# The narrow tile of the mixer shares its chunks with the third pooled tile; row totals, pooling weights and v's turn at other places of the queues

## The reference

```python
mod = (silu(c) @ ada_w + ada_b).reshape(B, 3, 3, 1024)
shift, scale, gate = mod[:, :, 0], mod[:, :, 1], mod[:, :, 2]
h = rms_norm(x, norm_g[0]) * (1 + scale[:, 0]) + shift[:, 0]
x = x + 0.5 * gate[:, 0] * swiglu(h, ffn1_w_in, ffn1_w_out)
h = rms_norm(x, norm_g[1]) * (1 + scale[:, 1]) + shift[:, 1]
x = x + gate[:, 1] * token_mixer(h, mix_w_in, conv_w, a_log, dt_bias, ..., pool_w, pool_scale, pool_proj, ...)
h = rms_norm(x, norm_g[2]) * (1 + scale[:, 2]) + shift[:, 2]
x = x + 0.5 * gate[:, 2] * swiglu(h, ffn2_w_in, ffn2_w_out)
return rms_norm(x, final_g)
```

## Time and profile before

| | us |
|---|---|
| median of 3 runs | 1915.85 (1915.74 to 1916.16) |
| the profiled execution | 1915.09 |
| its span in the profile | 1913.3 |
| PE busy | 1873.1 (98%) |
| DVE busy | 988.9 (52%) |
| ACT busy | 815.8 (43%) |
| POOL busy | 124.2 (6%) |

### The profile page before, as it was taken

The page is one execution under the profiler, slowest core; times in us unless marked ns, Lnnn a source line. Parts: engine busy times, 40 slices in busy tenths (PEclk is TensorE's granted clock), DMA queues, the critical chain, the costliest instruction groups (busy, mean ns, idle before and its releaser), DMA issues.

```text
span 1913.3 us, 22366 instructions
## 1 busy us (share of the span) xinstructions
PE 1873.1 (98%) x8923; PEld 1452.5 (76%) x8923; DVE 988.9 (52%) x1764; ACT 815.8 (43%) x1325; POOL 124.2 (6%) x148
## 2 busy tenths in 40 slices
PE   7999999999999999999999999999999999999997
PEld 4666666666788788888886777677888878888886
DVE  4566667666544643333347566854434673333322
ACT  5466556656643342222324555434432342222221
POOL 0111111110001000000010011000000100000000
PEclk9999999999999999999999999999999999999999
DMA  5334334332233132222223222221023322322221
GB/s 213 147 144 150 137 143 155 143 144 99 78 118 123 69 110 99 94 96 92 99 95 117 93 72 88 84 94 34 34 96 113 121 89 99 99 93 97 97 93 62
DMA packets 56526, 201.95 MB, mean 106 GB/s; under 512 B 6478, under 2 KB 6934, under 8 KB 55784
## 3 DMA queue, kind: packets, MB, share of 16 engines
q1 hardware_dynamic: 44616, 158.32, 23.6%
q0 software_dynamic: 11808, 42.21, 6.1%
HBM read 195.23 MB, written 5.28 MB: 105 GB/s over the span
## 4 chain that ended last, share of the span: by engine, by line
PE 76%; DVE 12%; ACT 9%; issue 2%; DMA 1%; POOL 0%; DVEq 0%; SPq 0%; ACTq 0%
PE ps L1111 22%; PE ps L1114 22%; PE ps L1112 22%; ACT wH L1820 2%; DVE wL L1404 2%; PE ps L1209 2%; PE ps L1173 1%; DVE a L1533 1%; PE ps L1197 1%; DVE a L1699 1%; ACT a L1931 1%; PE ps L1185 1%; PE ps L1245 1%; PE ps L1144 1%; DVE b L1464 1%
## 5 line engine op out<-in xcount | busy, mean ns | idle before, releaser
L1111 PE MATMUL ps<-hH,wH 128*128 128x512 f32 x1592 | 649.3, 408 | 7.6 <-ACT wH L1820 5.9
L1114 PE MATMUL ps<-hH,wL 128*128 128x512 f32 x1592 | 623.7, 392 | 0.2 <-DVE wL L1404 0.2
L1112 PE MATMUL ps<-hL,wH 128*128 128x512 f32 x1592 | 622.6, 391 | 0.0
L1404 DVE TENSOR_TENSOR wL<-wr,wH 128x1024 fp32r<-128x1024 f32 (+2 forms) x285 | 345.1, 1212 | 526.7 <-ACT wH L1820 526.5
L1820 ACT ACTIVATE wH<-wr 128x1024 fp32r<-128x1024 f32 (+2 forms) x285 | 295.0, 1036 | 239.8 <-PE ps L1114 226.1
L1111 PEld LDWEIGHTS ps<-hH,wH 128*128 128x128 f32 x1592 | 299.7, 188 | 104.6 <-issue 36.2
L1114 PEld LDWEIGHTS ps<-hH,wL 128*128 128x128 f32 x1592 | 299.0, 188 | 66.2 <-DVE wL L1404 1.1
L1112 PEld LDWEIGHTS ps<-hL,wH 128*128 128x128 f32 x1592 | 300.0, 188 | 62.6 <-issue 6.2
L1111 PE MATMUL ps<-gffn,wH 128*128 128x512 f32 x400 | 157.4, 394 | 1.0 <-DVE xT L1618 1.0
L1112 PE MATMUL ps<-gffn,wH 128*128 128x512 f32 x400 | 156.3, 391 | 0.0
L1114 PE MATMUL ps<-gffn,wL 128*128 128x512 f32 x400 | 156.2, 390 | 0.0
(11 more groups left out here) (301 smaller groups left out, 2049.6 us busy)
## 6 DMA issues: line engine op xcount, KB each, us to landing
wr<-wst SPq DMA_DIRECT2D x268, 512.0 KB, 3.5
a<-wfd POOLq DMA_DIRECT2D x54, 512.0 KB, 4.7
xT<-wfd POOLq DMA_DIRECT2D x18, 512.0 KB, 7.0
wr<-wst SPq DMA_DIRECT2D x16, 384.0 KB, 3.0
xT<-xin SPq DMA_DIRECT2D x8, 256.0 KB, 4.9
xT<-xin SPq DMA_DIRECT2D x2, 1024.0 KB, 6.1
xsave<-xT SPq DMA_DIRECT2D x1, 2048.0 KB, 7.9
c<-wfd POOLq DMA_DIRECT2D x8, 256.0 KB, 3.1
```

Of the source, the lines that this page charges most:

```text
L1111: e.matmul(o, hi, xh[k], start=k == 0, stop=False)
L1112: e.matmul(o, hi, xl[k], start=False, stop=False)
L1114: i = e.matmul(o, lo, xh[k], start=False, stop=k == t.nk - 1)
L1404: e.tensor_tensor(dst, x, hi.bitcast(F32), ALU.subtract).then_inc(s[name], 1)
```

## The change

- The row totals move from the sublayer ahead into raw_start, at k = 6, in all three openings. There the first tile's groups k = 6 and 7 are done together, before the second tile's.
- In the mixer norm_c is done in three pieces, chunks 0 to 3, 4 to 6 and 7, instead of two.
- feed_pool stands ahead of the mixer's raw_start and waits for other counts (the last al 22, and the row totals' copy) instead of hL.
- The narrow tile and pooled tile 2 share the chunks: narrow k = 0 to 3, pooled k = 0 to 3, then k = 4 to 7 in turn.
- pool_mid(0) moves from pooled tile 2 to pooled tile 3, pool_mid(1) to tick 3, (2) from tick 7 to 9, (3) from 15 to 16. So the narrow tile's turn stands ahead of pool_mid(0).
- v_turn stands two ticks later; the queries' l2_sum, l2 and prep_q one tick later.

```diff
--- before.py
+++ after.py
@@ -219,7 +219,12 @@
             if k == 2:
                 self.last_square()
                 self.raw(n, 7)
-            self.add("mm", t=t0, k=k)
+            if k == 6:
+                self.shift_sum(n, len(tiles))
+            if k < 7:
+                self.add("mm", t=t0, k=k)
+            if k == 6:
+                self.add("mm", t=t0, k=7)
             self.add("mm", t=t1, k=k, raw=self.sig("rm") if k < 7 else None)
         if t2 is not None:
             self.slot(t2, 0)
@@ -229,10 +234,13 @@
             t.done = t.slots[-1] + 1
         rs = self.sig("rs")
         self.add("norm_rs", n=n, stat=8 + 2 * n, rs=rs)
-        self.add("norm_c", n=n, c0=0, c1=5, rs=rs, raw=t1)
+        first, second = (4, 7) if n == 2 else (5, 8)
+        self.add("norm_c", n=n, c0=0, c1=first, rs=rs, raw=t1)
         self.add("split", j=t0.slots[0] + NSPL)
-        self.add("norm_c", n=n, c0=5, c1=8, rs=rs, raw=t1)
+        self.add("norm_c", n=n, c0=first, c1=second, rs=rs, raw=t1)
         self.add("split", j=t1.slots[0] + NSPL)
+        if n == 2:
+            self.add("norm_c", n=n, c0=7, c1=8, rs=rs, raw=t1)
         for name in ("nv", "nh", "nl"):
             self.count[name] = self.count.get(name, 0) + 8
         for i, t in enumerate(tiles):
@@ -459,7 +467,7 @@
         more = {4: [lambda: add("mod_rest"), lambda: self.raw(1, 0), lambda: self.raw(1, 1)],
                 5: [lambda c=c: self.raw(1, c) for c in (2, 3, 4)], 6: [lambda: self.raw(1, 5)], 7: [lambda: self.raw(1, 6)]}
         at = {(6, 9): lambda: self.shift_row(1, 0, first), (7, 1): lambda: self.shift_row(1, 1, first + 1),
-              (7, 8): lambda: self.shift_row(1, 2, first + 2), (7, 13): lambda: self.shift_sum(1, 3)}
+              (7, 8): lambda: self.shift_row(1, 2, first + 2)}
         for c in range(8):
             r = sig("xr")
             t = Tile("res0", src("l0_w_out", 128 * c, 16), self.pb01.take()[1], "g", ("xr", r), c=c, xr=r)
@@ -516,8 +524,6 @@
                         self.raw(2, c - 1)
                 if n == 1 and c == 7 and k in (2, 9):
                     self.shift_row(2, k // 9, first + k // 9)
-                if n == 1 and c == 7 and k == 16:
-                    self.shift_sum(2, 2)
         self.last_square = lambda: square(7)
         if n == 3:
             square(7)
@@ -541,18 +547,19 @@
         def pool_mid(g):
             add("pool_mid", g=g, bank=wk.take()[1], pm=sig("pm"), ya=sig("ya"), pd=g + 1)
 
+        add("feed_pool", done=self.count["wb"] + 1)
         self.raw_start(n, pool(0, "r"), pool(1, "r"))
-        add("feed_pool")
-        t = Tile("ba", src("mix_w_in_2", 4608, cols=16), wk.take()[1], "h", ("bd", 1), n=n)
-        self.whole(t)
-        for k in self.steps_of(pool(2)):
-            if k == 5:
-                pool_mid(0)
+        ba = Tile("ba", src("mix_w_in_2", 4608, cols=16), wk.take()[1], "h", ("bd", 1), n=n)
+        second = pool(2)
+        self.slot(ba, 0)
+        self.slot(second, 0)
+        for t, k in [(ba, k) for k in range(4)] + [(second, k) for k in range(4)] + [(t, k) for k in range(4, 8) for t in (ba, second)]:
+            self.mm(t, k)
         add("baturn", bank=wk.take()[1])
         self.move("saved")
         for k in self.steps_of(pool(3)):
             if k == 5:
-                pool_mid(1)
+                pool_mid(0)
         clock, events, n_ev = [0], [], [0]
 
         def at(tick, fn, *a):
@@ -619,7 +626,7 @@
                     at(clock[0] + 2, lambda: add("conv_taps", **d))
                     at(clock[0] + 7, conv_act, a)
                     if which == "v":
-                        at(clock[0] + 13, v_turn, h)
+                        at(clock[0] + 15, v_turn, h)
                 yield k
 
         def l2_sum(h, l2s):
@@ -677,22 +684,24 @@
 
             l2s = []
             for j, h in enumerate(hs):
-                at(end + 13 + j, l2_sum, h, l2s)
+                at(end + (13 if which == "k" else 14) + j, l2_sum, h, l2s)
                 if which == "k":
                     at(end + 19 + 2 * j, prep_x, h)
                     at(end + 36 + 2 * j, prep_k, h)
                 else:
-                    at(end + 38 + 2 * j, prep_q, h)
-            at(end + 17, l2, which, l2s)
+                    at(end + 39 + 2 * j, prep_q, h)
+            late = 0 if which == "k" else 1
+            at(end + 17 + late, l2, which, l2s)
             at(end + 26, l2_end, which, l2s)
 
         session(32, "k", range(4))
         session(76, "k", range(4, 8))
         session(120, "q", range(4))
         session(164, "q", range(4, 8))
-        at(7, pool_mid, 2)
+        at(3, pool_mid, 1)
+        at(9, pool_mid, 2)
         at(11, lambda: add("decays", bank=wk.take()[1]))
-        at(15, pool_mid, 3)
+        at(16, pool_mid, 3)
         at(123, lambda: add("sol_send", pa2=8))
         for k in range(1, 31):
             at(135 + 3 * k, lambda k=k: add("solve", k=k))
@@ -798,8 +807,6 @@
             self.raw(3, c)
             if 3 <= c < 6:
                 self.shift_row(3, c - 3, first + c - 3)
-            elif c == 6:
-                self.shift_sum(3, 3)
 
         for c in range(8):
             r = sig("xr")
@@ -2171,7 +2178,8 @@
                     for j in range(ADA_BUFS):
                         ada_feed(d["at"] + ADA_BUFS + j)
                 elif what == "feed_pool":
-                    w.wait_ge(s["nl"], 24)
+                    w.wait_ge(s["al"], 22)
+                    w.wait_ge(s["wb"], d["done"])
                     pool_feed()
                     pool_feed()
                 elif what == "pool_mid":
```

## The result

The changed kernel takes **1925.57 us** (median of 4 runs, 1925.05 to 1925.88), the kernel before 1915.8 (1914.41 to 1916.16): 9.8 us more, a ratio of 1.0054 (95% interval 1.0039 to 1.0069). Forecast were 1921 and at most 1925. The sign is right; the size is not, it is nearly twice the forecast of 5.3, and the time lies .57 above the upper end of the forecast range.

What follows compares the result with a forecast made beforehand. PE, busy 98% of the span, was taken to bound the kernel, so only its waits and clock could move the time: -1.6 + 6.8 - 2.0 + 2.1 = +5.3 on 1915.85 gave 1921.1, said as 1921 us; range 1916 to 1925.

Steps and rivals of the forecast that it cites:

- Step 1: ffn1's opening: shift-row wait and half clock go, .35 bank wait and 1.45 norm_c stall come; -1.6 us.
- Step 2's turn: Mixer's opening: PE idles 6.8 us at the narrow tile's turn, waiting for DVE's copy of that tile.
- Step 4: ffn2's opening: uncovered row totals +.63 and the norm_c block +1.45; +2.1 us.
- The clock behind the turn: Mixer's opening: the clock falls low after the turn's 6.8 us wait; +1.7 us.
- rival B: Clock costs more: two low stretches at the mixer (3.4), one in ffn2 (1.7); +8.7, 1924.5 us; chance .17.
- step 2: Mixer's opening as a whole: delay 5.1 plus clock 1.7; +6.8 us, ends 6.0 and 8.5.
- behind it stand pool(3) and pool_mid(0), whose input is long there: Mixer: pool_mid(0) now lies behind the narrow tile's turn, adding .86 us to the delay.
- step 3: Queries and v: waits for squares shrink 1.4, v's wait for o .6; -2.0 us, between -1.4 and -2.75.
- A: Totals' copy doesn't hold DVE up: 1913.6, or 1911.9 without a slow mixer stretch; chances .10 and .05.
- C: Clock costs less (full after the long wait) or waits regained elsewhere: 1918.8, down to 1917.7; chance .15.
- The split of norm_c and the earlier pooling weights in themselves: Mixer's opening: both hidden under the turn's wait, so worth nothing.

Runs made afterwards that it cites:

- a_sum_old: Changed kernel with the row totals back at their old places in the sublayer ahead; 1922.18 us, 1.0035 against the kernel before.
- b_qv: Kernel before with only the queries' steps one tick later and v's turn two ticks later; 1914.98 us, ratio .9998.
- a_turn: Changed kernel with the narrow tile's turn moved ahead of pooled tile 3's last group (k = 7); 1918.59 us, 1.0018 against the kernel before.
- b_mid: Kernel before with only the pool_mids at the changed kernel's places, the turn still ahead of pooled tile 3; 1918.77 us, ratio 1.0019.
- b_feed: Kernel before with only the pooling weights fetched earlier, ahead of the opening; 1913.42 us, ratio .9991.
- best3: best2 plus the change's later ticks for queries and v, and the inverses two ticks later; 1908.08 us, .9962 against the kernel before.
- best4: best3 with the mixer's norm_c in two pieces again and the inverses one more tick later; 1906.65 us, .9954 against the kernel before.
- a_sum2: Changed kernel with the row totals at k = 2 of the openings instead of k = 6; 1919.81 us, 1.0024 against the kernel before.
- a_mid_old: Changed kernel with pool_mid(0) back in front of the narrow tile's turn, at pooled tile 2's k = 5; 1921.5 us, 1.0034 against the kernel before.
- b_sum: Kernel before with only the row totals moved to k = 6 of the three openings; 1919.55 us, ratio 1.0024.
- best2: Changed kernel with ffn1's totals at k = 2, others at old places, turn later, pool_mid(0) and (1) earlier, old query and v ticks; 1911.04 us, .998 against before.

## Why the prediction was wrong

Right were, by its own steps:

- **Step 1, ffn1**: -1.6 forecast, -1.5 measured. The wait for the shift row is gone, and the block of norm_c is there: DVE's copy waits 7.90 for PE's totals, and PE stalls 1.6 over the following tile (1.45 forecast), beginning with .37 for wL. The low clock behind the shift row's wait is gone too, but the forecast put that down to the edit, and the runs don't show it: in a_sum_old and b_qv, whose ffn1 is that of before, it is absent as well behind the same wait of 1.70, and PE's difference falls by 1.2 there without an edit. So some 1.2 of this step's gain can be luck.

```profile
660.44 0.17 DVE L1477 COPY tiny<-ps 128x6 f32<-128x6 f32 x1 [7.90 <-PE ps L1135]
660.52 1.40 DVE L1486 SCALAR_TENSOR_TENSOR affn<-xT,tiny,affn 128x512 f32<-128x512 f32 x2
...
674.20 1.22 DVE L1411 TENSOR_TENSOR wL<-wr,wH 128x1024 fp32r<-128x1024 f32 x1 [0.20 <-ACT wH L1827]
```

- **Step 2's turn**: forecast were a wait of 6.8 and a place 4.25 late, measured 6.63 and 4.2 (2.55, and 1.6 that ffn1 gave).
- **Step 4, ffn2**: 2.1 forecast, 2.2 measured; PE's wait for xT grew from .98 to 1.61 as forecast, and the totals and the stall follow. The clock stayed full.

```profile
1548.91 0.50 PE L1118 MATMUL ps<-gffn,wH 128*128 128x512 f32 x1 [1.61 <-DVE xT L1625]
...
1558.30 0.72 PE L1135 MATMUL ps<-cst,b 128*128 128x2 f32 x6
...
1568.14 0.50 PE L1121 MATMUL ps<-hH,wL 128*128 128x512 f32 x1 [0.37 <-DVE wL L1411]
```

Wrong were:

- **The clock behind the turn was mis-sized.** The sum had 1.7, for 3.40 us of half clock. But the row that it names shows more: the second line of the earlier trace rows, behind the 5.8 us of idle PE, is 5.90 us at .50. Here PE was at half clock for 6.0 us, and from the turn to the pool_mid six groups behind it PE took 7.30 (1047.51 to 1054.81), where before it took 4.57 (1044.96 to 1049.53): 2.7. The prediction had two low stretches only as an end of its range and as rival B. With 2.7 step 2 gives 5.1 + 2.7 = 7.8, and 8.1 was measured; .3 stays open.
- **"behind it stand pool(3) and pool_mid(0), whose input is long there", priced at .86.** This is the step of the prediction that failed. It followed PE's way alone and priced pool_mid(0) as PE's work. It didn't ask who waits for pool_mid(0): ACT, which can't take out pooled tile 2 before, and behind that tile DVE, the decays, and the first key. The chain lost 3.1 us by norm_c (DVE's weights split ahead of pooled tile 2 ends at 1048.58, before at 1045.44) and 7.7 by the wait of 7.97 instead of .26, together 10.86. PE met it in the keys: +3.8, for which the sum had no term. a_turn shows the first part alone (chain 3.13 late), b_mid the second alone (5.84 by the pool_mids' places, with its stage .7 earlier than in before).
- **"Sum -2.0", step 3.** The waits shrank, by 2.6. But b_qv shows that it is given back at the solve's data, 1.48 there and 1.74 in the changed kernel:

```profile
1282.43 1.75 PE L1295 MATMUL ps<-cst,a 128*128 128x128 f32 x14 [1.74 <-DMA a<-dsol]
```

  The prediction didn't ask what is late next. The 1.5 us of the slow clock at 1303, which the trace of after lacks, hide most of this error in the total.

Of the rivals, A is out (the copy does wait, 7.45 and 7.90), B is right in its first half (clock at the mixer) and wrong in ffn2, where the clock stayed. C's long wait at full clock didn't occur. "The split of norm_c and the earlier pooling weights in themselves ... worth nothing" holds for the weights (b_feed); the third piece costs: from norm_c's start to the narrow tile's copy DVE takes 24.33 us in best3 and 22.68 in best4, which has two pieces, and best4's first key is 1.3 earlier although its stage began .3 later. In the changed kernel, where norm_c starts late, the piece cost about the .8 forecast (23.42 from norm_c's start to the copy's, before 22.68).

## What to carry to other kernels

When a step is moved on the busiest engine, list who reads what it frees, not only who stands behind it in the queue: here a product of .9 us was the gate of a buffer on another engine. When an engine with slack against a chain is delayed, price the chain and the engine apart and take the later one at the place where they meet; a wait of .37 us at such a place, as at the keys' last square sum before, says that they already touch. A copy that waits for a late place of another engine belongs behind the work that doesn't need it.

## What the runs showed of the hardware

- In the changed kernel PE worked at half clock for 6.0 us (1047.5 to 1053.5) behind 6.63 us of idle time; at the program's start in before it was 5.9 us behind 5.8. After 1.97 us of idle at the turn (b_mid) the clock also fell (.74 in 1045.4 to 1048.8); after 2.28 (b_feed) and .99 (a_turn) it stayed at 1.00. So the length of one wait doesn't tell whether it falls.
- The same wait of 1.50 us before the solve's small matmuls (1301 to 1303 in before) was followed by the half clock in before (.50), b_qv and a_turn, and by the full clock in the changed kernel, a_sum_old, a_sum2, a_mid_old, b_mid, b_sum, b_feed and best2. 1.5 us come and go with it, whatever the change. The line for before; a_turn's is above:

```profile
1303.90:1307.30 3.40, 3.40 (x40) 2.75 (x31) 1.37 (x2) 1.22 (x2) 0.00 (x0) 0.50 0.02 5
```

- The same holds at two places on which the prediction drew. Behind ffn1's wait of 1.7 for the shift row the clock was at .50 in before, b_mid and b_feed, and full in a_sum_old and b_qv (b_qv's line below).

```profile
652.70:656.10 3.40, 3.31 (x14) 2.38 (x14) 2.58 (x3) 2.19 (x3) 0.00 (x0) 1.00 0.03 7
```

- Behind the mixer's waits of 1.12 and .58 for hL, from which rival B argued, the clock fell to .54 in before. In b_feed it stayed full behind the same two waits, with PE busy as much ahead of it:

```profile
1031.00:1034.00 3.00, 1.29 (x5) 0.32 (x5) 2.59 (x5) 2.00 (x4) 0.00 (x0) 1.00 0.00 0
1034.00:1037.60 3.60, 3.53 (x16) 2.31 (x15) 2.61 (x5) 1.54 (x2) 0.00 (x0) 1.00 0.70 291
```

- PE waited 1.47 us for the pooling weights in before and 2.87 in b_qv, with the same steps up to there.
- One kernel's executions spread over 3.8 us (before, 1913.1 to 1916.9) on longer measuring, more than the .4 of the first three runs told.
